# Four shared raw tiles, V and O without ones, gate weights and first mask a stage ahead, and one output product placed later

## The chip, the cores and the metric

The program runs on one core of a Trainium2 chip. The metric is the time of one execution on the device in microseconds (us), the median of three runs. The engines are called as the profile calls them: PE (TensorE, matmul), PEld (its weight loads), DVE (VectorE), ACT (ScalarE), POOL (GpSimd), SP (the queue that issues most loads and stores).

## What is computed

A trunk of two layers over 2048 positions of width 1024, all in float32. Each layer normalizes h, scales and shifts it by a modulation worked out from c, mixes, and adds gate * y to h. Layer 0 is an S5 state space beside an mLSTM; layer 1 is sliding-window attention. The change lies in layer 0 and in what it prepares for layer 1. Cut to that:

```python
def adaln(c, w, b):                      # the modulation of a layer: shift, scale, gate
    m = jax.nn.silu(c) @ w + b
    return jnp.split(m[:, None, :], 3, axis=-1)

def s5_mixer(...):                       # y is the scan's output
    return y * jax.nn.sigmoid(y @ w_glu)

def mlstm_cell(q, k, v, log_i, log_f):   # one step of the scan over chunks of 128
    b = cumsum(lf)
    d_log = where(tri, b[:, None] - b[None, :] + li[None, :], -inf)
    m_t = maximum(b + m_st, max(d_log))
    s = (q @ k.T) * exp(d_log - m_t)
    g = exp(b + m_st - m_t)
    num = s @ v + g * (q @ c_st)
    den = sum(s) + g * (q @ n_st)
    h = num / maximum(abs(den), exp(-m_t))
    c_new, n_new = decay * c_st + (w_k * k).T @ v, decay * n_st + sum(w_k * k)

def mlstm_mixer(m_in, ...):
    xc = silu(causal_conv(m_in, conv_w, conv_b))
    q, k = xc @ wq, (xc @ wk) * M_HEAD_DIM ** -0.5       # by head, 4 heads of 256
    v, o = m_in @ wv, sigmoid(m_in @ wo)
    log_i, log_f = split(concat([xc, m_in]) @ w_if + b_if)   # log_f = log_sigmoid
    h = mlstm_cell(q, k, v, log_i, log_f)
    return rmsnorm(o * h, norm_g) + skip * xc

# layer 0:  h = x + gate * (concat([y_s5, y_m * silu(m_z)]) @ w_out)
```

## The kernel before

The program is a row of stages; between two of them all engines meet (`m.clear()`), and only what has been started ahead of that crosses. Within a stage each engine runs a program of its own, written out by hand, and waits for the others by semaphores. So the order of work on an engine, and of the loads on SP's queue, is the order of the code. Every float32 product of the large ones is made as three (high by high, high by low, low by high part); to get the parts ACT casts a raw tile to its high part and DVE subtracts that from the raw tile to get the low part. This pair is called a split below. One such product of 128x512 is one MATMUL row.

**glu** takes the scan's output y and gives y * sigmoid(y @ w_glu) times a SiLU, in four blocks of 512 positions; the result goes to DRAM as `ys_d`. Its tile `g_u` holds one input. At its end SP loads the weights of dense's head 0 into `m.wide` and the inputs of dense's unit 0 into the two tiles `m.bridge`, counted by the semaphore `m.ahead`.

**dense** has 16 units, four heads by four blocks of 512 positions. Unit u does 48 products: q, k, and v beside o, in eight groups that go through four PSUM banks `e_pg`; ACT reads each result into one of four `e_stage` tiles and stores it to `cq_d`, `ck_d` or `vo_d`. A `vo_d` row holds v (256), a one, and o (256): the one makes the cell's product with v give the sum `den` too, and ACT writes it for each result (L1682). After unit u stands tile u-1: 48 products of 128 positions of `ys_d` with the first half of `ev_w_out` (L1772 to L1774, banks `e_po`), which DVE scales by the gate row `e_gate` (L1742) and adds to x (L1746); SP stores it as `h0_d`. The eight rows of that weight (512 KB each) come through two raw tiles `m.second` (`out_weight`, L1582): from the third on, each load waits until a raw tile has been split. SP's order is: four weight rows, unit 1's inputs (L1565, L1566), y (L1571), the gate chain's transfers, four weight rows, and from then on for each u: unit u+1's inputs, y, head weights, the store of tile u-2, x, the gate chain's transfers, a piece of the second layer's modulation weight `ada_w` (L1590). POOL multiplies that piece by SiLU(c) and adds it to `ada_sum` (L1634). The class `Gates` (L1385) works out the cell's decays from the gate logits in parts, one for each unit; part 2 is a long chain of small DVE instructions behind unit 2, for whose result SP waits before it goes on with unit 4's inputs.

In DVE's and ACT's programs unit u+1's splits stand ahead of tile u-1's residual. The last y (tile 15) is cast into `e_y`, the same tile that tile 14's products read, so ACT's cast waits for these (L1659), and the last product uses the banks `e_po` again, which DVE must have read.

**cell** is the mLSTM in 16 chunks of 128 positions by 4 heads. For each head PE does `first` (turns the keys, makes the scores and the product q @ state) and `second` (the state's update and scores @ v); DVE and ACT do the masking, the normalizing and the state. `turn(c)` transposes a chunk's heads, `y_part` and `blend` (DVE, ACT) make y_m of it, and `outputs(c, n)` multiplies it in 24 products with the second half of `ev_w_out` (L2272), of which each chunk has two. The eight rows of that weight come through the two tiles `m.bridge`; DVE multiplies each by the gate row (`fold`, L2154) before it is split (L1976, L2148), one for each head of chunks 0 and 1. The stage begins with 48 products by ones that sum `ada_sum` (L2279), an addition and a transpose of the second layer's gate row, which ACT copies and SP stores; the loads of weights 2 to 5 wait on SP for that. POOL makes the causal mask at the start, and for each chunk mask minus `gate_run`, of which ACT takes exps. The keys and queries of chunk 0 are loaded into `m.second` at dense's end, v and o into `m.wide`.

Chunk 0's `turn` and `outputs(0, 0)` stand in chunk 1: the turn behind `second(1, 0)`, the product behind `second(1, 2)`; DVE's blend of chunk 0 stands ahead of head 2 of chunk 1.

## Time and profile before

| what | value |
|---|---|
| median of three runs | 3034.83 us |
| the three runs | 3034.83, 3031.55, 3037.38 us |
| the profiled execution, its own time | 3025.52 us |
| its span in the trace | 3023.7 us |
| PE busy | 2765.6 us (91%) |
| DVE, ACT, POOL busy | 1558.9, 1103.1, 640.8 us |
| mean granted clock of PE | 0.957 |
| dense, from its first product to its last | 1234.8 to 1629.8 us |
| cell, first product | 1636.7 us |

The profile is of one execution. Its own time is 1.8 us more than its span, which is what lies around the span, and 9.3 us less than the median of the three runs. Busy times are sums over the span; what a change in one stage is worth has to be read from the stretch of that stage, from which engine waits there and for what. A granted clock of 1.00 is PE's full 2.4 GHz; a mean of 0.75 over a stretch is a mixture of that and of 1.2 GHz. A row of a timeline gives the start and length of an instruction (or of a run of like ones, xN), and in brackets how long its engine had been idle before it and whose end released it.

### The profile page before, as it was taken

How to read it: one execution, taken by the hardware profiler on the slowest of the kernel's cores; microseconds unless marked ns; L12 is line 12 of the kernel's file. 1: busy time of each engine (PE TensorE's matmuls, PEld its weight loads, DVE VectorE, ACT ScalarE, POOL GpSimd, SP SyncE). 2: the span in 40 equal slices, each digit the busy share in tenths (PEclk: the TensorE clock that was granted, in tenths of full speed). 3: DMA queues.
4: the chain of work that ended last, by engine and by line, in shares of the span. 5: the costliest groups of instructions: out<-in, count | busy, mean ns of one | idle time of the engine just before them, and what ended most of it. 6: DMA issues, size and time to landing. Idle time of an engine off the chain costs nothing. (4 is left out here: it accounts for less than half of the span.)

```text
span 3023.7 us, 36865 instructions
## 1 busy us (share of the span) xinstructions
PE 2765.6 (91%) x13163; PEld 2195.2 (73%) x13163; DVE 1558.9 (52%) x3227; ACT 1103.1 (36%) x2442; POOL 640.8 (21%) x526
## 2 busy tenths in 40 slices
PE   4799998999999799689997699997899999899999
PEld 2677887888888678578785577776677777667776
DVE  5565771556655456453223666664534431456664
ACT  2611221222222222334331455553522222366664
POOL 0004661544545100032232000000100000033332
PEclk7899999999999899899998899999899999999999
DMA  7216446454454465698896465662422324512221
GB/s 252 95 67 149 146 145 155 138 149 144 147 157 138 151 218 178 211 251 238 256 276 193 133 178 168 165 171 79 167 73 74 88 76 122 166 60 89 85 85 63
DMA packets 454027, 445.66 MB, mean 147 GB/s; under 512 B 157556, under 2 KB 349388, under 8 KB 450380
## 3 DMA queue, kind: packets, MB, share of 16 engines
q1 hardware_dynamic: 350340, 337.75, 38.0%
q10 hardware_dynamic: 103504, 105.54, 10.8%
q8 instruction: 106, 1.74, 0.2%
q14 instruction: 77, 0.63, 0.1%
HBM read 282.06 MB, written 162.74 MB: 147 GB/s over the span
## 5 line engine op out<-in xcount | busy, mean ns | idle before, releaser
L2771 PE MATMUL a_pg<-a_hT,a_whl 128*128 128x512 f32 x640 | 256.7, 401 | 3.4 <-DVE a_whl L878 3.4
L2772 PE MATMUL a_pg<-a_hT,a_whl 128*128 128x512 f32 x640 | 251.1, 392 | 0.0
L2773 PE MATMUL a_pg<-a_hT,a_whl 128*128 128x512 f32 x640 | 250.9, 392 | 0.0
L884 PE MATMUL p_g<-hT,w_hl 128*128 128x512 f32 x512 | 212.2, 415 | 0.0
L830 PE MATMUL pg<-hT,w_hl 128*128 128x512 f32 x512 | 206.3, 403 | 6.5 <-DVE w_hl L878 6.5
L832 PE MATMUL pg<-hT,w_hl 128*128 128x512 f32 x512 | 201.9, 394 | 0.0
L831 PE MATMUL pg<-hT,w_hl 128*128 128x512 f32 x512 | 201.7, 394 | 0.0
L886 PE MATMUL p_g<-hT,w_hl 128*128 128x512 f32 x512 | 200.2, 391 | 0.0
L885 PE MATMUL p_g<-hT,w_hl 128*128 128x512 f32 x512 | 199.8, 390 | 0.0
L2771 PEld LDWEIGHTS a_pg<-a_hT,a_whl 128*128 128x128 f32 x640 | 121.4, 190 | 42.0 <-DVE a_whl L878 11.4
L2773 PEld LDWEIGHTS a_pg<-a_hT,a_whl 128*128 128x128 f32 x640 | 121.3, 189 | 26.3
L2772 PEld LDWEIGHTS a_pg<-a_hT,a_whl 128*128 128x128 f32 x640 | 121.6, 190 | 23.6
L1074 POOL TENSOR_TENSOR s_region<-s_wt 128x512 f32<-128x512 f32 x64 | 72.5, 1133 | 299.7 <-DMA s_wt<-s5w_d 299.5
L1094 DVE TENSOR_TENSOR s_region<-p_v,s_region 128x512 f32<-128x512 f32 x64 | 44.1, 690 | 162.9 <-PE p_v L1172 154.8
L2272 PE MATMUL xp_o<-x_wout,x_yhl 128*128 128x512 f32 x256 | 108.8, 425 | 14.8 <-DVE x_wout L2148 9.6
L2920 POOL TENSOR_TENSOR shared<-shared,b_stat 128x1024 f32<-128x1024 f32 x43 | 81.5, 1896 | 184.2 <-DVE b_stat L2987 184.2
L1349 PE MATMUL g_ps<-g_gh,g_w 128*128 128x512 f32 x256 | 101.6, 397 | 19.9 <-DVE g_gh L1259 15.4
L830 PEld LDWEIGHTS pg<-hT,w_hl 128*128 128x128 f32 x512 | 97.7, 191 | 29.6 <-DVE w_hl L878 7.3
L832 PEld LDWEIGHTS pg<-hT,w_hl 128*128 128x128 f32 x512 | 97.4, 190 | 21.0
L831 PEld LDWEIGHTS pg<-hT,w_hl 128*128 128x128 f32 x512 | 97.8, 191 | 19.2
L886 PEld LDWEIGHTS p_g<-hT,w_hl 128*128 128x128 f32 x512 | 96.2, 188 | 20.7
L885 PEld LDWEIGHTS p_g<-hT,w_hl 128*128 128x128 f32 x512 | 96.4, 188 | 19.9
(502 smaller groups left out, 6848.9 us busy)
## 6 DMA issues: line engine op xcount, KB each, us to landing
s_wt<-s5w_d SPq DMA_DIRECT2D x64, 354.0 KB
vo_d<-e_stage ACTq DMA_DIRECT2D x64, 256.5 KB, 8.5
w_raw<-in_ev_w_in SPq DMA_DIRECT2D x32, 512.0 KB, 5.7
s5w_d<-gate_sums SPq DMA_DIRECT2D x32, 512.0 KB, 3.0
shared<-h_d SPq DMA_DIRECT2D x28, 512.0 KB, 4.1
arena<-in_ada_w SPq DMA_DIRECT2D x8, 1536.0 KB, 11.6
e_ada_w<-in_ada_w SPq DMA_DIRECT2D x32, 384.0 KB, 7.4
a_raw<-in_od_w_in SPq DMA_DIRECT2D x40, 256.0 KB, 3.4
```

The costliest lines, as they stand in the source:

```text
L830: nc.tensor.matmul(out, w[:, 0, k, :], x[:, 0, k, :], start=(k == 0), stop=False)
L831: nc.tensor.matmul(out, w[:, 0, k, :], x[:, 1, k, :], start=False, stop=False)
L832: last = nc.tensor.matmul(out, w[:, 1, k, :], x[:, 0, k, :], start=False, stop=(k == KC - 1))
L884: nc.tensor.matmul(out, w(0, k), x(0, k), start=(k == 0), stop=False)
L885: nc.tensor.matmul(out, w(0, k), x(1, k), start=False, stop=False)
L886: last = nc.tensor.matmul(out, w(1, k), x(0, k), start=False, stop=(k == n - 1))
L1349: nc.tensor.matmul(ps[n][:], w(0), gh[:, 0, k, :], start=(k == 0), stop=False)
L2272: mm(O[n][:], yhl[:, 0, k, :], wo[:, 0, k, cols], start=(k == 0), stop=False)
L2771: mm(bank, w[:, 0, k, :], x[:, 0, k, :], start=(k == 0), stop=False)
L2772: mm(bank, w[:, 0, k, :], x[:, 1, k, :], start=False, stop=False)
L2773: last = mm(bank, w[:, 1, k, :], x[:, 0, k, :], start=False, stop=(k == KC - 1))
L2920: nc.gpsimd.tensor_tensor(p, p, st[G % 3][:, 4].unsqueeze(2).broadcast_to([P, 4, 2 * P]), ALU.mult).then_inc(p_ready, 1)
```

## The change

- A new shared tile `four` of 128x4096 (2 MB), with the views `m.row[0..3]`, lives from glu to cell. glu uses it for `g_u`, dense for four raw rows of its output weight, then for two rows of the cell's weight (`row[2]`, `row[3]`) and chunk 0's keys and queries (`row[0]`, `row[1]`). `m.second` is gone.
- At glu's end, when the last block's `g_u` is used up, SP also loads the first four weight rows of dense. In dense the other four come in one burst once the first four are split.
- `vo_d` has no column of ones, ACT no longer writes one, and the cell loads v and o in two pieces; POOL sets the column in the tiles once. The tiles for the gate row, the `ada_w` piece and the mask are shared from dense on, and several tiles now overlie others.
- The gate chain's part 2 is cut in two, "2" and "2b"; the second is behind unit 3's splits on DVE.
- In dense's last units SP loads four rows of the cell's weight, and DVE folds the gate into them there (units 14 and 15 and behind the last y). Chunk 0's inputs are loaded in unit 14. POOL subtracts and ACT takes the exps of chunk 0's mask (`m.pm0`) at dense's end.
- The last y goes into the tile `e_x`, and the last tile's products into two `e_pg` banks, half by half, each half with a signal of its own.
- In the cell, the products by ones stand behind `first(0, 1)`, the transpose behind `first(0, 3)`, and only rows 4 to 7 of the weight are loaded and folded, through four tiles. `turn(0)` stands behind `second(1, 2)`, blend and y_part of chunk 0 at chunk 1's end, and `outputs(0, 0)` behind `second(1, 3)`, in chunk 2.

```diff
 def glu: (at the end of SP's program)
+                sp.wait_ge(pre, NB * KC)
+                for k in range(4):
+                    sp.dma_start(m.row[k], a["ev_w_out"][0, k * P:(k + 1) * P, :]).then_inc(m.ahead_w, 16)
...
 def dense:
+        ylast = xhl[:].rearrange("p q k t -> p q (k t)").rearrange("p q (k t) -> p q k t", t=P)
+        y_of = lambda t: yhl[:] if t < LASTU else ylast
+        bank = lambda t, n: (po if t < LASTU else pg)[n][:]
...
                 def out_weight(k):
-                    if k >= 2:
-                        sp.wait_ge(wo_lo, k - 1)
-                    sp.dma_start(wo_raw[k % 2][:], wov[k]).then_inc(wo_in[k % 2], 16)
+                    sp.wait_ge(wo_lo, KC // 2)
+                    sp.dma_start(wo_raw[k % 4], wov[k]).then_inc(wo_in, 16)
...
-                for k in range(KC // 2):
-                    out_weight(k)
                 unit(1)
                 y(0)
...
+                    if u in (UNITS - 4, UNITS - 3):
+                        k = u - UNITS + 4
+                        sp.dma_start(m.row[2 + k], next_wov[k]).then_inc(m.ahead_w, 16)
+                    if u == UNITS - 2:
+                        next_inputs()
+                sp.wait_ge(u_lo, 2 * UNITS)
+                for k in range(2):
+                    sp.dma_start(m.bridge[k][:], next_wov[2 + k]).then_inc(m.ahead_w, 16)
+                modulation(LASTU)
...
+                pool.wait_ge(m.ahead, 16 * 11)
+                pool.wait_ge(causal_ready, 2)
+                pool.wait_ge(gates.moved, 16)
+                nc.gpsimd.tensor_tensor(m.pm0, m.causal[:].unsqueeze(1).broadcast_to([P, MH, MC]), m.gb[:], ALU.subtract).then_inc(masked, 1)
...
                 def y(t):
                     act.wait_ge(y_in, 16 * (t + 1))
-                    if t:
+                    if t == LASTU:
+                        act.wait_ge(u_done, UNITS)
+                    elif t:
                         act.wait_ge(t_done, t)
-                    nc.scalar.copy(yhl[:, 0], y_raw[:]).then_inc(y_hi, 1)
+                    nc.scalar.copy(y_of(t)[:, 0], y_raw[:]).then_inc(y_hi, 1)
...
-                        nc.scalar.activation(s[:, HD:HD + 1], pg[g % 4][:, 0:1], ACT.Copy, scale=0.0, bias=1.0)
...
+                for h in range(MH):
+                    nc.scalar.activation(m.pm0[:, h, :], m.pm0[:, h, :], ACT.Exp, bias=m.gcol[:, 0, 0, h:h + 1]).then_inc(weighted, 1)
...
+                def fold(k):
+                    v.wait_ge(m.ahead_w, 16 * (6 if k < 2 else 8))
+                    raw = m.row[2 + k] if k < 2 else m.bridge[k - 2][:]
+                    tt(raw, raw, gate[:], ALU.mult).then_inc(folded, 1)
...
+                    if u == 2:
+                        gates.vector(v, "2b")
+                    if u >= UNITS - 2:
+                        fold(u - UNITS + 2)
                 y(UNITS - 1)
+                for k in range(2, 4):
+                    fold(k)
                 residual(UNITS - 2)
                 residual(UNITS - 1)
+                v.wait_ge(folded, 4)
...
 def cell: (PE's program)
-                pe.wait_ge(ada_ready, 1)
-                nc.tensor.transpose(O[1][0:KC, 0:P], m.ada[:, 1, 2 * KC:3 * KC], m.ident[:]).then_inc(gate_turned, 1)
                 for c in range(NMC):
                     first(c, 0)
                     if c:
                         second(c - 1, MH - 1)
+                    if c == 2:
+                        outputs(0, 0)
                     first(c, 1)
+                    if c == 0:
+                        modulation()
                     second(c, 0)
                     if c >= 2:
                         outputs(c - 2, 1)
-                    if c:
                         turn(c - 1)
...
                     second(c, 2)
-                    if c:
+                    if c == 1:
+                        turn(0)
+                    if c >= 2:
                         outputs(c - 1, 0)
```

Three places show how instructions move. First SP's queue from glu's end into dense; `UNCONDITIONAL_BRANCH` is the border of the stages, `e_y_raw` the y of tile 0, `t_bias` and `gt_d` the gate chain's. Before (the border stands right above):

```order
L1585 DMA second<-in_ev_w_out 128x1024 x4
L1565 DMA bridge<-xc_d 128x2x512
L1566 DMA bridge<-m_d 128x2x512
L1571 DMA e_y_raw<-ys_d 128x1024
L1414 DMA t_bias<-in_m_b_if 8x1
L1416 DMA gt_d<-gate_sums 8x2048
L1585 DMA second<-in_ev_w_out 128x1024 x4
L1599 DMA e_gate<-gate_d 128x1024
L1576 DMA e_h<-in_x 128x1024
L1590 DMA e_ada_w<-in_ada_w 64x1536 x2
L1565 DMA bridge<-xc_d 128x2x512
```

and after:

```order
L1323 DMA four<-in_ev_w_out 128x1024 x4
L1280 UNCONDITIONAL_BRANCH
L1564 UNCONDITIONAL_BRANCH
L1574 DMA bridge<-xc_d 128x2x512
L1575 DMA bridge<-m_d 128x2x512
L1580 DMA e_y_raw<-ys_d 128x1024
L1416 DMA t_bias<-in_m_b_if 8x1
L1418 DMA gt_d<-gate_sums 8x2048
L1593 DMA four<-in_ev_w_out 128x1024 x4
L1616 DMA gate_row<-gate_d 128x1024
L1585 DMA e_h<-in_x 128x1024
L1598 DMA ada_w<-in_ada_w 64x1536 x2
```

Four rows of the weight moved ahead of the border, and unit 1's inputs and the bias are the first loads of dense.

Second, DVE at dense's end, up to its last instruction. `e_y<-e_y_raw` is the split of the last y, the pairs on `e_up` and `e_h` are the residuals of tiles 14 and 15. Before:

```order
L1708 TENSOR_TENSOR e_y<-e_y_raw,e_y 128x1024
L1742 TENSOR_TENSOR e_up<-e_po,e_gate 128x512 x2
L1746 TENSOR_TENSOR e_h<-e_h,e_up 128x512 x2
L1708 TENSOR_TENSOR e_y<-e_y_raw,e_y 128x1024
L1742 TENSOR_TENSOR e_up<-e_po,e_gate 128x512 x2
L1746 TENSOR_TENSOR e_h<-e_h,e_up 128x512 x2
L1742 TENSOR_TENSOR e_up<-e_po,e_gate 128x512 x2
L1746 TENSOR_TENSOR e_h<-e_h,e_up 128x512 x2
```

and after, where `gate_sums` is the tile that `e_up` now overlies and `gate_row` the gate:

```order
L1771 TENSOR_TENSOR four<-four,gate_row 128x1024
L1743 TENSOR_TENSOR e_y<-e_y_raw,e_y 128x1024
L1785 TENSOR_TENSOR gate_sums<-e_po,gate_row 128x512 x2
L1789 TENSOR_TENSOR e_h<-e_h,gate_sums 128x512 x2
L1771 TENSOR_TENSOR four<-four,gate_row 128x1024
L1743 TENSOR_TENSOR e_x<-e_y_raw,e_x 128x1024
L1771 TENSOR_TENSOR bridge<-bridge,gate_row 128x1024 x2
L1785 TENSOR_TENSOR gate_sums<-e_po,gate_row 128x512 x2
L1789 TENSOR_TENSOR e_h<-e_h,gate_sums 128x512 x2
L1785 TENSOR_TENSOR gate_sums<-e_pg,gate_row 128x512 x2
L1789 TENSOR_TENSOR e_h<-e_h,gate_sums 128x512 x2
```

Four folds (L1771) came in, two of them between the last split and the residuals, the last split writes `e_x`, and the last residual reads `e_pg` banks.

Third, PE at the cell's start. `xp_ks` and `xp_bb` are `first`, `xp_c` and `xp_aa` are `second`, `xp_o<-ones` the products by ones. Before:

```order
L2279 MATMUL xp_o<-ones,ada_sum 128x1 x24
L2284 MATMUL xp_o<-ident,ada 8x128
L2226 MATMUL xp_ks<-ident,second 128x128 x2
L2228 MATMUL xp_ks<-second 128x128 x2
L2235 MATMUL xp_bb<-x_c,second 128x257 x2
L2226 MATMUL xp_ks<-ident,second 128x128 x2
L2228 MATMUL xp_ks<-second 128x128 x2
L2235 MATMUL xp_bb<-x_c,second 128x257 x2
L2245 MATMUL xp_c<-wide,x_kw 128x257
```

and after:

```order
L2287 MATMUL xp_ks<-ident,four 128x128 x2
L2289 MATMUL xp_ks<-four 128x128 x2
L2298 MATMUL xp_bb<-x_c,four 128x257 x2
L2287 MATMUL xp_ks<-ident,four 128x128 x2
L2289 MATMUL xp_ks<-four 128x128 x2
L2298 MATMUL xp_bb<-x_c,four 128x257 x2
L2343 MATMUL xp_o<-ones,ada_sum 128x1 x24
L2308 MATMUL xp_c<-wide,x_kw 128x257
L2309 MATMUL xp_c<-wide,x_kw 128x257
L2313 MATMUL xp_aa<-wide,x_st 128x257
```

The products by ones moved behind the second `first`, and the transpose (L2284 before) has left this stretch.

## Rows read from the trace of the kernel before

**Rows 1.** Windows, all engines: window, its length, busy (x instructions) by engine, clock, DMA.
```profile
1234.80:1295.00 60.20, 39.44 (x150) 31.64 (x151) 21.88 (x19) 24.37 (x47) 6.17 (x2) 0.81 0.77 246
1295.00:1629.80 334.80, 322.53 (x1391) 264.87 (x1390) 116.90 (x152) 122.58 (x274) 95.42 (x30) 0.98 0.85 242
1642.50:1716.00 73.50, 40.46 (x163) 31.73 (x164) 41.45 (x91) 30.78 (x75) 5.68 (x3) 0.74 0.59 178
```

**Rows 2.** Timeline of PE in dense: its first instruction after each wait.
```profile
1260.80 0.79 PE L1772 MATMUL e_pg<-e_x,e_wh 128*128 128x512 f32 x1 [12.54 <-DVE e_x L1708]
...
1292.39 0.80 PE L1772 MATMUL e_pg<-e_x,e_wh 128*128 128x512 f32 x1 [8.22 <-DVE e_x L1708]
...
1318.37 0.50 PE L1772 MATMUL e_pg<-e_x,e_wh 128*128 128x512 f32 x1 [1.41 <-DVE e_x L1708]
...
1476.65 0.79 PE L1772 MATMUL e_pg<-e_x,e_wh 128*128 128x512 f32 x1 [4.23 <-DVE e_x L1708]
...
1616.04 0.77 PE L1772 MATMUL e_po<-e_wout,e_y 128*128 128x512 f32 x1 [5.97 <-DVE e_up L1742]
```

**Rows 3.** DMA issues of 1380 to 1600: KB each, median us to landing.
```profile
bridge<-m_d SPq DMA_DIRECT2D x9, 512.0 KB, 12.3
```

**Rows 4.** Timeline of DVE at glu's end.
```profile
1215.59 1.16 DVE L1277 TENSOR_TENSOR g_o<-g_s,g_z 128x512 f32<-128x512 f32 x1 [3.63 <-DMA ys_d<-g_o]
```

**Rows 5.** Timelines of SP, DVE and ACT at dense's start.
```profile
1231.17 13.97 SPq L1585 DMA_DIRECT2D second<-in_ev_w_out  x4
...
1258.19 1.27 DVE L1453 TENSOR_SCALAR gate_sums<-gate_sums,t_bias 8x2048 f32<-8x2048 f32 x1 [3.76 <-DMA t_bias<-in_m_b_if]
...
1272.75 0.86 SPq L1565 DMA_DIRECT2D bridge<-xc_d  x1
...
1288.75 1.04 ACT L1648 CAST e_x<-bridge 128x1024 fp32r<-128x1024 f32 x1 [10.31 <-DMA bridge<-m_d]
```

**Rows 6.** Timelines at dense's end and the border to cell.
```profile
1610.16 1.04 ACT L1659 CAST e_y<-e_y_raw 128x1024 fp32r<-128x1024 f32 x1 [9.99 <-PE e_po L1774]
...
1611.24 3.46 DVE L1708 TENSOR_TENSOR e_y<-e_y_raw,e_y 128x1024 fp32r<-128x1024 f32 x1 [14.06 <-ACT e_y L1659]
...
1630.05 1.29 DVE L1742 TENSOR_TENSOR e_up<-e_po,e_gate 128x512 f32<-128x512 f32 x2 [10.90 <-PE e_po L1774]
...
1613.69 4.30 POOL L1634 TENSOR_TENSOR ada_sum<-ada_sum,e_ada_w 128x1536 f32<-128x1536 f32 x1
...
1636.72 5.28 PE L2279 MATMUL xp_o<-ones,ada_sum 64*128 64x1 f32 x48 [6.71 <-PEq L148]
```

**Rows 7.** Timelines of DVE, ACT and PE in cell's first two chunks.
```profile
1660.86 1.23 DVE L2154 TENSOR_TENSOR bridge<-bridge,x_gate 128x1024 f32<-128x1024 f32 x1 [5.86 <-DMA bridge<-in_ev_w_out]
...
1690.97 2.15 DVE L2126 SCALAR_TENSOR_TENSOR x_y<-xp_o,cols,x_xs 128x128 f32<-128x128 f32 x8
...
1695.43 1.23 DVE L2138 TENSOR_TENSOR x_yhl<-x_y,x_yhl 128x1024 fp32r<-128x1024 f32 x1
...
1664.54 0.42 ACT L1991 ACTIVATE x_ha<-x_hs 128x256 f32<-128x256 f32 x1 [10.06 <-DVE x_hs L2104]
...
1670.84 0.42 ACT L1991 ACTIVATE x_ha<-x_hs 128x256 f32<-128x256 f32 x1 [0.61 <-DVE x_hs L2104]
...
1707.98 0.76 PE L2272 MATMUL xp_o<-x_wout,x_yhl 128*128 128x512 f32 x1 [9.64 <-DVE x_wout L2148]
...
1727.46 0.60 PE L2260 MATMUL xp_o<-ident,x_hs 128*128 128x128 f32 x4
```

**Rows 8.** Windows over one chunk each, in the cell's middle.
```profile
1757.32:1783.00 25.68, 24.14 (x122) 19.80 (x121) 16.14 (x50) 15.24 (x38) 1.89 (x2) 1.00 0.63 177
1860.06:1886.83 26.77, 24.14 (x122) 19.79 (x121) 17.22 (x50) 15.24 (x38) 1.26 (x1) 1.00 0.56 170
```

**Rows 9.** Timelines of SP and ACT: unit 10's second input.
```profile
1457.23 0.70 SPq L1566 DMA_DIRECT2D bridge<-m_d  x1
...
1474.29 1.04 ACT L1648 CAST e_x<-bridge 128x1024 fp32r<-128x1024 f32 x1 [8.97 <-DMA bridge<-m_d]
```

252 lines of the change are left out of this document (146 added, 106 removed).

## The prediction

> **What bounds the kernel now.** I read the windows by stage first, then TensorE's (PE's) timeline, then what the engine that released it was doing. PE carries the program; the three stages that the change touches are glu (up to 1231) [rows 5], dense (1234.8 to 1629.8) and cell (from 1636.7). In dense PE is busy 322.5 of 334.8 us once it runs, but only 39.4 of its first 60.2 us, and 40.5 of the 73.5 us with which cell begins, at granted clocks of 0.81 and 0.74 where dense's middle has 0.98 [rows 1]. So there is nothing to win in the middle and much at two starts. PE's own idle stretches are few and long: 12.5, 8.2, 1.4, 4.2 and 6.0 us in dense [rows 2]. The other input is DMA: its share is 0.85 over dense's middle [rows 1], and a 512 KB input takes 12.3 us to land there [rows 3].
>
> **glu's end.** Four loads of 512 KB (rows of the output weight) go onto SP's queue behind those that are there. VectorE already waited 3.6 us for a store to land while such loads ran [rows 4]; 2 MB more prolong that by 6 to 8 us, and the last stores are then each late. I charge +1 us (0 to +4): two output tiles stand between VectorE and these stores and take up part of the delay, and a second wait as long as the one that is there is the upper end.
>
> **dense's start.** Before, SP spends 14.0 us on four weight loads, because two raw tiles must come free in turn, and only then issues unit 1's inputs; four more weights follow before unit 2's [rows 5]. Behind the first set stands also the bias, for which VectorE waits at 1258.2 [rows 5] ahead of unit 1's splits. PE finishes unit 0 at 1248.3 (1260.80 less 12.54) and starts unit 1 at 1260.8 [rows 2]. After, unit 1's inputs leave once unit 0's are split, near 1236, and are in before unit 0 ends. ScalarE (ACT), which must fit four weight casts between eight results, I put 1 us behind PE; the last result (0.8), a cast (1.0) and a split (1.2) follow, and PE goes on near 1252.7: a wait of 4.5 us. The last four weights now come in one burst that starts near 1250.5 and lands near 1259, and ACT stands before it with seven results behind it; PE has four banks in hand, so I charge 2.5 us (0 to 5). Unit 1 and tile 0 took 23.4 us (1260.80 to 1284.17), and unit 2 then waited 8.2 us for inputs issued at 1272.75, which landed 16 us later behind the weights [rows 2, 5]. After, these are issued near 1254.5 with 2 MB less ahead of them and land by 1268. Unit 2 starts at 1248.3 + 4.5 + 23.4 + 2.5 = 1278.7 and not at 1292.4: -13.7. A wait also costs a slow restart: tile 15 took 14.0 us from 1616.04 to 1630.05 [rows 2, 6] against 10.9 at full clock (1344 products from 1292.39 to 1610.07, less waits and restarts, 0.228 each, 48 to a unit or tile), so 3.1; unit 1 and tile 0 together show 1.6. For the restart that goes I take 2.4. Sum -16.1 (-10 to -19).
>
> **The gate chain.** In unit 2 the second part (about 7 us of small instructions) moves behind unit 3's splits. Unit 3's wait of 1.4 us [rows 2] goes. But SP stands at the store of this chain's result until it is done, and unit 4's inputs are queued behind: issued near 1309, needed by 1319. I charge +1 (0 to +5). Sum -0.4. Unit 10's wait (4.2) [rows 2] has none of its causes touched: 0 (-6 to 0).
>
> **The last units.** Rows of the next stage's weight (0.5 MB each) go into units 12 and 13, its chunk 0 inputs (2.2 MB) into unit 14, two rows more behind unit 15. Dense's DMA is busy 0.85 [rows 1], a unit moves some 5.3 MB (242 GB/s by 21.8 us), so 0.5 MB delay a landing by about 1.6 us. Of the units after unit 2 only unit 10 waited over 2 us [rows 2], so most have some time in hand. Cost 0 (0 to +6).
>
> **dense's end.** ACT waits 10.0 us for tile 14 before it can cast the last y, PE then waits 6.0 us [rows 2, 6]. After, the last y goes into the tile of unit 15's inputs and the last product into other banks: both are free long before, so PE goes on at 1610.1: -6.0, and its restart goes, -3.1. The last product is done half by half; one scaling (0.6) is hidden: -0.6. What is late next? The addition loads now stand behind two 0.5 MB rows, then GpSimd (POOL) adds (4.3) [rows 6], makes the mask (1.4), ACT does exps (2.6): about 1626 in before's clock, where the last store lands near 1627. Cover is 1 us thin: +1 (0 to +4). Sum -8.7.
>
> One thing speaks against this term: VectorE's last split took 3.46 us while POOL added, against 1.23 for an instruction of its size in cell [rows 6, 7], and the last two folds (two SBUF operands each) now stand in that place. At this row's excess of 2.2 each the sum would have +4.5. I take it as a rival, since tile 15's 10.9 us give the folds room. The Trainium skill, "SBUF — State Buffer", section "SBUF: two separate sides", says that VectorE's and GpSimd's shared port pair is an exclusive lock and the loser blocks for the whole instruction; by that rule the sum would have one POOL instruction's length for every fold that comes second. The row agrees that there is a price, though it is shorter than the POOL addition beside it.
>
> **cell's start**, in t from the stage's first PE instruction (1636.72). Before, 48 products by ones, an addition and a transpose (5.8 us) precede all else; the first output product starts at t = 71.3, the second ends at t = 90.7 [rows 7]. VectorE paces it. Its heads follow at 6.3 us where fold, split and cast of a weight chain through ACT (1664.54 to 1670.84), and it stands 5.9 us for a weight load (1660.86) [rows 7], as the two raw tiles and SP's wait for the gate row hold the loads back. After: the mask, its exps and four folds are done in dense; POOL's memsets hold the first bank product until t = 2.2; the ones-products stand behind first(0,1) and end near 10.6, so head 0 is put out at 13.8. Then, by my count of each head's instructions, the heads: 5.2 (no fold), 6.3, 5.0, 6.3, 8.3 (with chunk 0's normalisation), 5.2, so t = 50 for the seventh. The last weight split (1.2) and the blend with its cast and split (1690.97 to 1696.66, 5.7) [rows 7] give t = 57 for the first output product, by which time first(2,0) and second(1,3) are done. It runs 7.0 with its restart, then 2.8 of recurrence and 5.6 of the second product: t = 72.4. -18.3 (-11 to -22). The moved loads of weights 4 to 7 leave SP at t = 10 and 22 and are needed at 22 and 33, with landings of 6 to 8 us: hidden. The split vo load adds one issue (0.8 us) to an SP queue that waits most of the time: 0.
>
> **cell's middle.** Chunks take 25.7 us, or 26.8 when POOL's subtraction meets VectorE (DVE busy 16.1 or 17.2) [rows 8]. The phase may shift either way: 0 (-6 to +6).
>
> **The sum**: +1 - 16.1 - 0.4 - 8.7 - 18.3 = -42.5. Against the profiled span of 3023.7 that is 2981.2, and 2983.0 for its own time of 3025.5. That run is 9.3 below the median of the runs shown, so I forecast 3034.8 - 42.5 = 2992.3 for a median.
>
> **Rivals.**
> - *Dense is bound by DMA.* For: share 0.85, over 1 in stretches. If bytes and not waits set the stage, its gain goes and glu's and cell's stay: -17, 3018. Against: PE does run 1295 to 1629.8 at 322.5 busy, and after it needs only 9% more rate. 0.12.
> - *The early work only moves the chain.* ACT's hand-overs, not loads, set cell's first two chunks: only the 5.8 at the head and the 5.9 wait less 5.8 of ones-products are saved, -6 in place of -18.3: 3004. For: the 6.3 pace has no DMA in it. Against: seven heads at 5 to 8 us still end by 50. 0.10. Both of these together give 3029, within 0.2%: 0.03.
> - *VectorE held up by POOL* in the last two folds, as above, +4.5: 2997. For: the row of 3.46. Against: nothing waits for these folds until cell's first output product. 0.05.
> - *Slower: input landings in dense.* One mechanism: loads packed closer in time make each unit's input late, as unit 10's was (ACT waited 9.0 us for it, and it landed 17.1 us after its issue) [rows 9]. Price 4.2 of idle and 2.4 of restart, 6.6; on twelve units 79, less 42.5: 3071. It decides from seven such units on, that is when the median landing of 12.3 us [rows 3] passes about 17. Against: only one unit in fourteen did. 0.05.
>
> **Numbers.** Forecast 0.65, about 2974 to 3010 by itself. Each case but the last two is faster by over 0.2%, about what a measurement can tell from no change: faster 0.92, same 0.03, slower 0.05. The range reaches over the bounds of start and cell (-61 would need all best ends) and up to the DMA case: 2974 to 3018.
>
> **What would show it.** PE's idle before unit 1 near 4.5 us and none before unit 2; no idle before tile 15; cell's first output product at t = 57, waiting for the split of y and not for a weight; dense's length 371 and not 402. Wrong if unit inputs are waited for in several units, if POOL's or ACT's last work ends dense, or if glu ends over 4 us later.

## The result, and the profile after

The changed kernel takes 2991.7 us (median, 2991.0 to 2998.3) where the kernel before took 3036.1 beside it. The ratio worked out from all runs is 0.9865, interval 0.985 to 0.988; that of the two medians is 0.9854. The forecast was 2992.3. The profiled execution of the changed kernel has a time of its own of 2991.0 and a span of 2989.2, so the two traces shown differ by 34.5 us, and the medians by 44.4. The forecast's sum was made against the first of these. The total is therefore nearer than its terms deserve, and the terms are what follows.

Each stretch below is taken from PE's timelines, from the start of one product to the start of another, so that it doesn't matter that the changed run was already 2.0 us late before glu's first product.

| stretch | before | after | difference | forecast |
|---|---|---|---|---|
| glu's first product to dense's first | 192.7 | 193.9 | +1.2 | +1 |
| to unit 3's first product | 83.6 | 65.8 | -17.8 | -17.5 |
| unit 3 to unit 5 | 43.7 | 52.2 | +8.5 | +1 |
| unit 5 to unit 9 | 88.4 | 87.7 | -0.7 | 0 |
| unit 9 to unit 11 | 50.6 | 43.5 | -7.1 | 0 |
| unit 11 to unit 15 | 87.1 | 87.1 | 0 | 0 |
| unit 15 to dense's last product | 41.5 | 33.0 | -8.5 | -9.7 |
| to the cell's first product | 7.1 | 10.3 | +3.2 | +1 |
| to the end of the second output product | 90.7 | 71.8 | -19.0 | -18.3 |
| to the last chunk's output product | 370.2 | 372.5 | +2.3 | 0 |
| everything else | | | +3.4 | 0 |

Of the +3.4 of everything else 2.0 stand ahead of glu's first product and 1.4 behind the last chunk's output product.

The windows over the same places as [rows 1] (window, its length, then busy time and count of PE, PEld, DVE, ACT and POOL, granted clock, DMA share, GB/s):

```profile
1237.98:1298.20 60.22, 54.16 (x216) 43.54 (x217) 34.04 (x38) 28.63 (x50) 12.64 (x4) 0.90 0.87 290
...
1280.00:1607.60 327.60, 319.96 (x1402) 263.38 (x1402) 153.79 (x160) 122.35 (x221) 98.23 (x30) 0.99 0.86 260
...
1617.50:1691.00 73.50, 57.47 (x270) 46.60 (x271) 44.20 (x115) 35.72 (x85) 5.82 (x6) 0.80 0.64 175
```

In dense's first 60 us PE is busy 54.2 and not 39.4, at a clock of 0.90 and not 0.81; at the cell's start it is 57.5 and not 40.5. PE's timeline, the first instruction behind each of its long waits (start, length, instruction, and the wait with its releaser), answers to [rows 2, 6, 7]:

```profile
1256.97 0.80 PE L1822 MATMUL e_pg<-e_x,e_wh 128*128 128x512 f32 x1 [5.19 <-DVE e_x L1743]
...
1332.68 0.79 PE L1822 MATMUL e_pg<-e_x,e_wh 128*128 128x512 f32 x1 [6.90 <-DVE e_x L1743]
...
1617.51 0.66 PE L2287 MATMUL xp_ks<-ident,four 128*128 128x128 f32 x2 [9.88 <-PEq L148]
...
1673.42 0.79 PE L2335 MATMUL xp_o<-x_wout,x_yhl 128*128 128x512 f32 x1 [6.62 <-DVE x_yhl L2197]
```

Unit 1 waits 5.2 us (12.5 before), units 2, 3 and 10 and tile 15 don't wait. Two waits are new or longer: 6.9 ahead of unit 4, and 9.9 at the border to the cell, where there were 6.7. The first output product comes 55.9 us behind the cell's first product and waits for the split of y.

**Unit 4.** Its chain in the timelines of SP and ACT (`mx_d` is the store of the gate chain's part 2, `bridge` the inputs):

```profile
1312.04 0.65 SPq L1426 DMA_DIRECT2D mx_d<-t_ends  x1
...
1314.65 0.47 SPq L1575 DMA_DIRECT2D bridge<-m_d  x1
...
1329.33 1.05 ACT L1677 CAST e_x<-bridge 128x1024 fp32r<-128x1024 f32 x1 [13.74 <-DMA bridge<-m_d]
```

SP issued unit 4's inputs only after the store for whose data it had stood, they landed 14.7 us later, and PE, idle from 1325.8, wanted them 3.5 us before ACT could begin to cast them.

**The border.** DVE and POOL at dense's end; the last product starts at 1607.2:

```profile
1603.85 6.79 DVE L1789 TENSOR_TENSOR e_h<-e_h,gate_sums 128x512 f32<-128x512 f32 x2
1610.84 1.29 DVE L1785 TENSOR_TENSOR gate_sums<-e_pg,gate_row 128x512 f32<-128x512 f32 x2 [0.20 <-DVE e_h L1789]
...
1603.50 2.75 POOL L1656 TENSOR_TENSOR ada_w<-ada_w,c_silu 128x1536 f32<-128x1536 f32 x1 [8.88 <-DMA ada_w<-in_ada_w]
1606.33 3.76 POOL L1659 TENSOR_TENSOR ada_sum<-ada_sum,ada_w 128x1536 f32<-128x1536 f32 x1
1610.05 1.71 POOL L1663 TENSOR_TENSOR gate_sums<-causal,gate_run 128x512 f32<-128x512 f32 x1
```

The two additions of tile 14's residual take 6.8 us beside POOL's two instructions, 1.3 without such company (in combo2, below). So the last residual starts 3 us later than the last product allows, and with it the last store.

### The profile page after: what moved, and what is told of

The parts are those of the page before. It is cut to its first block and busy times, and to the rows that moved or that the text cites. A ratio compares the mean times of both kernels' runs of the same rounds, so it can differ in the third digit from the quotient of the medians.

```text
span 2989.2 us, 36821 instructions
## 1 busy us (share of the span) xinstructions
PE 2758.0 (92%) x13163; PEld 2190.9 (73%) x13163; DVE 1586.3 (53%) x3227; ACT 1099.1 (37%) x2378; POOL 640.4 (21%) x528
## 3 DMA queue, kind: packets, MB, share of 16 engines
q8 instruction: 106, 1.74, 0.2%
## 5 line engine op out<-in xcount | busy, mean ns | idle before, releaser
L2844 PEld LDWEIGHTS a_pg<-a_hT,a_whl 128*128 128x128 f32 x640 | 121.7, 190 | 26.4
L831 PEld LDWEIGHTS pg<-hT,w_hl 128*128 128x128 f32 x512 | 97.8, 191 | 19.1
L886 PEld LDWEIGHTS p_g<-hT,w_hl 128*128 128x128 f32 x512 | 96.5, 189 | 20.8
## 6 DMA issues: line engine op xcount, KB each, us to landing
ada_w<-in_ada_w SPq DMA_DIRECT2D x32, 384.0 KB, 8.2
```

Source lines behind the costliest of these rows:

```text
L831: nc.tensor.matmul(out, w[:, 0, k, :], x[:, 1, k, :], start=False, stop=False)
L886: last = nc.tensor.matmul(out, w(1, k), x(0, k), start=False, stop=(k == n - 1))
L2844: last = mm(bank, w[:, 1, k, :], x[:, 0, k, :], start=False, stop=(k == KC - 1))
```

## The experiments

All are edits of the changed kernel, but for the last. Medians were taken with the kernel before at 3042 to 3046 us in these comparisons, where the result had 3036, and the changed kernel was not timed again beside them; so stretches of the traces are compared first. "Dense" is from its first product to the cell's first: 402.0 before, 379.5 after.

One trace of each has a scatter of its own. Three of the experiments below leave dense's code alone (pool_phase, output_old, ones_first), and their dense is 380.3, 381.5 and 382.1; so 379.5 is the low end of a band of 2.6 us, and a difference of that size shows nothing. At the cell's start, the seven traces with the changed kernel's code there have the first output product at t = 53.9 to 55.9 from the cell's first product, and the second's end at 70.3 to 72.1.

**s_behind: SP's store of the chain behind unit 4's inputs.**

```diff
                     if u + 1 < UNITS:
                         unit(u + 1)
+                    if u == 3:
+                        gates.transfers(sp, 2)
                     y(u)
...
-                    gates.transfers(sp, u)
+                    if u != 2:
+                        gates.transfers(sp, u)
```

> The changed kernel, with one edit: the store that waits for the gate chain's part 2 is issued by SP behind unit 4's inputs and not ahead of them. In the changed kernel PE waits 6.9 us ahead of unit 4 (1332.68). Theory (SP's order): its inputs left SP only at 1314.0, since SP stood at that store until VectorE's chain was done at 1312; with the edit they leave near 1305, the wait is gone, and with its restart dense is 8 to 10 us shorter (about 370 from its first to the cell's first product, where the changed kernel has 379.5). Rival (bytes): these inputs needed 15 us to land because the queues are full; leaving earlier they land hardly earlier, a wait of 4 us or more stays, and dense gains under 3 us.

Dense 378.2, median 2991.5 (2986.1 to 2996.0): 1.3 us less than 379.5, which is no more than the scatter, and not 8 to 10. Unit 4 does not wait any more, so the cause was named rightly; but its price came back one step later, which neither theory had. PE, then DVE and POOL:

```profile
1317.87 0.77 PE L1825 MATMUL e_po<-e_wout,e_y 128*128 128x512 f32 x1 [5.26 <-DVE gate_sums L1788]
...
1304.54 7.88 DVE L1469 SCALAR_TENSOR_TENSOR t_w<-t_w 64x128 f32<-64x128 f32 x7
...
1304.98 2.77 POOL L1659 TENSOR_TENSOR ada_w<-ada_w,c_silu 128x1536 f32<-128x1536 f32 x1 [10.24 <-DMA ada_w<-in_ada_w]
1307.84 3.50 POOL L1662 TENSOR_TENSOR ada_sum<-ada_sum,ada_w 128x1536 f32<-128x1536 f32 x1
```

Tile 2 waits for the residual of tile 1, which stands behind the chain on DVE, and the chain is long: seven instructions take 7.9 us while POOL works, and the same seven take 2.2 in the changed kernel, where SP's stall had kept POOL's data away by chance:

```profile
1306.85 2.19 DVE L1469 SCALAR_TENSOR_TENSOR t_w<-t_w 64x128 f32<-64x128 f32 x7
```

**chain_whole: part 2 in one piece again.**

```diff
                     gates.vector(v, u)
+                    if u == 2:
+                        gates.vector(v, "2b")
...
-                    if u == 2:
-                        gates.vector(v, "2b")
```

> The changed kernel with the gate chain's part 2 in one piece again, behind unit 2's work, as before the change. Theory (the cut trades one wait for another): the chain ends near 1306 and not 1312, unit 4's inputs leave 6 us earlier and its wait of 6.9 falls to about 0 to 1; but unit 3's splits come 7 us later and unit 3 waits about 7: dense 379.5 give or take 2. Rival (the cut is a gain by itself and unit 4 waits for something else): 7 to 10 us longer. Second rival (the cut is a loss by itself, since VectorE has time in hand in unit 2): 7 us shorter.

Dense 377.7, median 2993.7. Unit 3 waits 5.3 us, unit 4 not at all: the cut in two traded one wait for another, as the first theory said; what it was worth by itself is too little to see here (1.8 us).

**chain_slot3: both queues cleared.**

```diff
                     gates.vector(v, u)
+                    if u == 3:
+                        gates.vector(v, "2b")
...
-                    if u == 2:
-                        gates.vector(v, "2b")
...
                     x(u)
-                    gates.transfers(sp, u)
+                    if u == 3:
+                        gates.transfers(sp, 2)
+                    if u != 2:
+                        gates.transfers(sp, u)
```

> The changed kernel with the gate chain's second piece one unit later on VectorE (behind the residual of tile 1, ahead of unit 4's splits) and SP's store of its result behind unit 3's loads, so that neither unit 4's inputs nor tile 2's residual stand behind it. With the store alone moved (s_behind) unit 4's wait of 6.9 us went, but tile 2 then waited 5.3 us for a residual behind the chain, whose row of seven instructions took 7.9 us while POOL added the modulation. Theory (two queues, SP's and VectorE's, have to be cleared both): no wait over 2 us in units 3 to 5 and their tiles, dense 7 to 9 us shorter than 379.5. Rival (the chain costs wherever it stands, since POOL's instructions hold it): a wait of 4 to 6 us ahead of unit 4, whose splits are now behind it, dense within 2 us of 379.5.

Dense 373.4, 6.2 us shorter and clear of the scatter; median 2987.4 (2985.3 to 2988.4). Units 3 to 5 and their tiles don't wait; two waits of 1.1 and 1.2 us turned up later in the stage. The chain itself was not disturbed there (L1469 took 2.2 us); POOL fell on the residual ahead of it, whose two additions took 7.0 us, and there DVE had the time.

**mod_early: the modulation one unit earlier from unit 8 on.**

```diff
-                    if u > 1:
-                        modulation(u - 1)
+                    if 1 < u < UNITS // 2:
+                        modulation(u - 1)
+                    if u == UNITS // 2:
+                        modulation(u - 1)
+                        modulation(u)
+                    if u > UNITS // 2:
+                        modulation(u)
...
-                modulation(LASTU)
                 store(UNITS - 2)
```

> The changed kernel with the pieces of the second layer's modulation weight loaded one unit earlier from unit 8 on, so that POOL has nothing of it left to do at dense's end. In the changed kernel VectorE's two additions of tile 14's residual take 6.8 us beside POOL's last two instructions, the last residual starts at 1610.8, 3 us behind PE's last product, and from that product to the cell's first one 9.9 us pass (before: 6.7). Theory (VectorE is held up by POOL at dense's end): the additions take 1.3 to 2.5 us and 9.9 falls to about 6.5, dense 3 us shorter. Rival (the mask's subtraction and its exps end the stage): 9.9 falls by 1 at most, unless these come earlier too; then the last store alone is left and both theories meet, and the length of the two additions tells them apart.

The border fell from 9.9 to 6.1 us and the two additions to 1.3, as the first theory has it. Still the kernel lost: dense 384.0, median 2999.1. Two pieces one behind the other made SP wait until POOL had used the first, and unit 9's inputs stood behind that:

```profile
1421.16 16.75 SPq L1598 DMA_DIRECT2D ada_w<-in_ada_w  x4
```

PE then waited 5.2 us ahead of unit 9 (at 1451.64). This was my own edit, and it repeats the mistake of the prediction: a wait on SP is paid by what is queued behind it.

**pool_phase: POOL's mask subtraction in each of the cell's chunks 7 us later.**

```diff
                     if c >= 2:
-                        pool.wait_ge(st_ready, seq(c - 1, 0))
+                        pool.wait_ge(hs_ready, seq(c - 1, 1) + 1)
```

> The changed kernel with POOL's mask subtraction of each chunk of the cell released by head 1's output of the chunk ahead and not by head 0's mask product, so about 7 us later in the chunk, where VectorE is idle for 2 us. In the changed kernel a chunk takes 26.1 to 26.8 us (from 1707.94 to 2024.75: twelve chunks, 26.4 each); before, four chunks took 25.7. Theory (the phase of POOL's subtraction against VectorE's split of y makes the difference): all chunks take about 25.7, the cell is 7 to 9 us shorter. Rival (the chunk is paced by PE or by ACT): no change within 2 us.

Every chunk but the last takes 25.67 us, the stretch from the cell's first product to the last chunk's output product is 8.0 us shorter (436.3 and not 444.3), and the median is 2983.1 (2981.1 to 2985.6). Windows of one chunk each, first two of the changed kernel and then two of pool_phase (columns as above):

```profile
1761.17:1787.25 26.08, 24.13 (x121) 19.79 (x121) 16.52 (x50) 15.24 (x39) 1.27 (x1) 1.00 0.57 172
1787.25:1813.53 26.28, 24.40 (x121) 19.87 (x121) 16.74 (x50) 15.24 (x39) 2.06 (x1) 1.00 0.56 171
```

```profile
1761.37:1787.04 25.67, 24.14 (x121) 19.80 (x121) 16.13 (x50) 15.24 (x39) 1.29 (x1) 1.00 0.56 170
1787.04:1812.71 25.67, 24.13 (x120) 19.79 (x121) 16.14 (x50) 15.23 (x39) 1.30 (x1) 1.00 0.59 177
```

PE, PEld and ACT are busy as long as before; DVE is busy 16.1 and not 16.5 to 16.7, and the chunk is shorter by that and no more. In the changed kernel POOL's instruction stood on the split of y:

```profile
1773.43 1.63 DVE L2197 TENSOR_TENSOR x_yhl<-x_y,x_yhl 128x1024 fp32r<-128x1024 f32 x1
...
1772.70 1.27 POOL L2021 TENSOR_TENSOR x_pm<-causal,gate_run 128x512 f32<-128x512 f32 x1 [24.81 <-DVE x_st L2138]
```

The split takes 1.6 us there and 1.2 alone.

**rows_late: the first four weight rows at dense's start and not at glu's end.**

```diff
-                sp.wait_ge(pre, NB * KC)
-                for k in range(4):
-                    sp.dma_start(m.row[k], a["ev_w_out"][0, k * P:(k + 1) * P, :]).then_inc(m.ahead_w, 16)
...
+                for k in range(4):
+                    sp.dma_start(m.row[k], a["ev_w_out"][0, k * P:(k + 1) * P, :]).then_inc(m.ahead_w, 16)
                 unit(1)
```

> The changed kernel with the first four rows of dense's output weight loaded at dense's start, ahead of unit 1's inputs, and not at glu's end (four raw tiles all the same, so SP does not wait between them). Theory (dense's start: what stands ahead of unit 1's inputs costs, at 2 MB by 240 to 300 GB/s some 7 to 8 us): unit 1's wait, 5.2 in the changed kernel, becomes 9 to 13, glu ends about 1 us earlier, and dense is 5 to 9 us longer than its 379.5. Rival (the four tiles alone are the gain, since they take SP's 14.0 us of waiting away): unit 1's wait stays within 2 us of 5.2 and the total within 2 us.

Unit 1's wait is 7.0 us and not 5.2; it starts 20.8 us behind unit 0, where the changed kernel has 19.0 and the kernel before 26.0. So of 7.0 us won there the four tiles alone give 5.2, and glu's end is 0.6 shorter. For the wait that is the rival's case. For the total it is not: dense came out at 385.7, 6.2 us longer, which is the theory's number; median 2996.9. The waits of 7.7 ahead of unit 4 and of 10.4 at the border are no explanation, since the four traces with unchanged dense have 6.9 to 8.7 and 9.9 to 10.7 there. Of the 3.6 us beyond their longest dense, unit 1 has 1.8; for the rest I have no mechanism.

**last_tile_old: the last y and product in e_y and e_po.**

```diff
-        y_of = lambda t: yhl[:] if t < LASTU else ylast
+        y_of = lambda t: yhl[:]
-        bank = lambda t, n: (po if t < LASTU else pg)[n][:]
+        bank = lambda t, n: po[n][:]
...
                 def y(t):
-                    if t == LASTU:
-                        act.wait_ge(u_done, UNITS)
-                    elif t:
+                    if t:
                         act.wait_ge(t_done, t)
```

> The changed kernel with the last y and the last product in the tiles and banks of before (e_y, e_po, the halves not apart). Theory (the term of dense's end, 6.0 of idle, 3.1 of restart, 0.6 of a scaling): PE waits about 6 us ahead of tile 15 again and tile 15 takes 14.0 and not 10.9; of this 9 the part that was covered by POOL's and DVE's late work at the border (9.9 us there, 6.7 before) comes back, so dense is 5 to 9 us longer than 379.5. Rival (the border is set by POOL's last piece and the exps in any case): under 3 us longer.

Dense 388.8, 9.3 us longer, median 3000.9. The wait ahead of tile 15 is 10.7 us and not the 6 of before, since the folds, whose weight rows landed only at 1605.4, now stand ahead of the residual that frees the bank:

```profile
1605.39 2.36 DVE L1769 TENSOR_TENSOR bridge<-bridge,gate_row 128x1024 f32<-128x1024 f32 x2 [4.27 <-DMA bridge<-in_ev_w_out]
...
1609.09 0.77 PE L1818 MATMUL e_po<-e_wout,e_y 128*128 128x512 f32 x1 [10.69 <-DVE gate_sums L1781]
```

The folds at dense's end are free only with the other banks; the two edits belong together.

**output_old: chunk 0's turn, blend and first output product where they were.**

```diff
-                    if c == 2:
-                        outputs(0, 0)
                     first(c, 1)
...
-                    if c == 1:
-                        turn(0)
-                    if c >= 2:
+                    if c:
                         outputs(c - 1, 0)
```

(and DVE's and ACT's parts of it likewise)

> The changed kernel with chunk 0's turn, blend and first output product where they stood before (the product behind second(1, 2)); all else as changed. The changed kernel has its first output product 55.9 us and the end of the second 71.8 us behind the cell's first product. Theory (most of the cell's 19 us comes from what is no longer done at its start, and the move gives some 4 to 6 of them, since before it PE held first(2, 0) and second(1, 3) behind a product that waited for the last weight): the second product ends 4 to 6 us later than 71.8. Rival (only the move makes the gain possible): 10 us or more later. Second rival (the move gives nothing, VectorE paces all): within 1.5 us.

The first output product comes at t = 52.9, but the second ends at 74.5 and not 71.8: the move is worth 2.8 us, less than I had set. Median 2995.2.

**fold_in_cell: rows 0 to 3 loaded early, but folded in the cell.**

```diff
-                    if u >= UNITS - 2:
-                        fold(u - UNITS + 2)
...
-                        if 2 <= k < 6:
-                            fold(k + 2)
+                        if k + 1 < KC:
+                            fold(k + 1)
```

> The changed kernel with rows 0 to 3 of the cell's weight loaded in dense as changed, but multiplied by the gate row in the cell, one for each head as before; dense's VectorE has no folds. Theory (VectorE paces the cell's start: each of the four folds stands in it): the first output product comes 4 to 5 us later than 55.9 (three folds of 1.2 and the first one with its cast behind it), and dense's end is not shorter, since its folds were hidden. Rival (the folds at dense's end cost there too, VectorE beside POOL): dense 1 to 3 us shorter, so that the total is nearly the same.

The first output product comes 59.2 us behind the cell's first and not 55.9, the end of the second is 3.6 later; dense is 380.1, no shorter. Median 2999.7. The folds are hidden in dense and on the path in the cell. The trace also shows that they only settle which additions meet POOL at the border: without them tile 14's two took 1.3 us, but tile 15's took 4.1 beside POOL's last addition, and the wait there was still 9.0.

**ones_first: the products by ones ahead of the cell again.**

```diff
+                modulation()
+                pe.wait_ge(ada_ready, 1)
                 for c in range(NMC):
                     first(c, 0)
...
-                    if c == 0:
-                        modulation()
                     second(c, 0)
```

> The changed kernel with the 48 products by ones and the addition of the modulation ahead of everything in the cell, as before the change (the transpose stays behind first(0, 3)). Theory (these 5.8 us are put off the path by the move, since VectorE waits for POOL's memsets and ACT's casts there anyway for 2 to 3 us): first output product 3 to 6 us later than the 55.9 of the changed kernel. Rival (before as after they are on the path, as head 0's output at 13.1 against 15.1 shows little gain): under 2 us later.

First output product at t = 56.7 (55.9), second's end at 73.2 (71.8); median 2998.1, with dense 2.6 us longer in this trace for reasons that the edit doesn't touch. The rival holds: of the 5.8 us that I saw ahead of all else, 0.8 to 1.5 were worth something, and these are hardly more than the scatter. If the three edits on the cell don't overlap, the experiments add up to 3.6 + 2.8 + 1.5 = 7.9 of its 19.0 us. The other 11 are left over, and I put them down to what was not tried apart: the loads that no longer wait for two raw tiles and for the gate row (waits of 5.9 and 2.5 us of DVE in the trace of before), and chunk 0's mask and exps.

**combo2: chain_slot3, pool_phase and the modulation early without the stall.**

```diff
-                    if u > 1:
+                    if 1 < u <= 8:
                         modulation(u - 1)
...
                     y(u)
+                    if u == LASTU:
+                        modulation(LASTU)
...
+                    if 8 <= u < LASTU:
+                        modulation(u)
...
-                modulation(LASTU)
                 store(UNITS - 2)
```

(beside the diffs of the other two)

> chain_slot3 and pool_phase together, and the modulation's pieces loaded one unit earlier from unit 8 on without SP waiting for POOL (each at its unit's end, the last one behind the last y), so that POOL is done before dense's end. Theory: 8.8 us from the cell's chunks (25.67 each), 7 to 9 from units 3 to 5 and about 3.8 from the border to the cell (9.9 to 6.1), 2970 to 2974 in all. Rival (a wait that goes is followed by the next one): the chunks' 8.8 alone, about 2983.

2973.4 us (2971.4 to 2982.7), a ratio to the kernel before of 0.977 (0.9753 to 0.9787). The 0.9865 of the change was taken against a faster series of the kernel before (3036 and not 3046), so the two ratios overstate the difference; the medians themselves differ by 18.3 us, the spans of the two traces by 18.4. PE has one long wait left in dense, and then the border:

```profile
1258.80 0.79 PE L1828 MATMUL e_pg<-e_x,e_wh 128*128 128x512 f32 x1 [5.19 <-DVE e_x L1749]
...
1608.78 0.66 PE L2293 MATMUL xp_ks<-ident,four 128*128 128x128 f32 x2 [6.11 <-PEq L148]
```

Dense is 368.8 us, 10.7 less than the changed kernel, and the cell up to the last chunk's output product 436.0 and not 444.3. This version beats both.

**before_again: the kernel before once more, for a second trace.**

> The kernel before once more, for a second trace: its profiled execution of 3025.5 us was the shortest of those seen, the others lie between 3031 and 3056. Theory (unit inputs in dense land late in some executions): the extra 10 to 25 us stand in dense as waits of PE for DMA. Rival (the phase of POOL against VectorE in the cell): the chunks of 25.7 are 26.4. Second rival (clock): no stage has them, all stages are longer in proportion.

Its profiled execution took 3047.7 us, with a span of 3045.9: 22.2 more than the trace shown. Of these 15.0 stand in dense (417.0), 3.7 ahead of glu, 0.7 in glu and 3.1 in the cell. Units 9 and 11 wait:

```profile
1464.52 0.79 PE L1772 MATMUL e_pg<-e_x,e_wh 128*128 128x512 f32 x1 [3.77 <-DVE e_x L1708]
...
1517.94 0.79 PE L1772 MATMUL e_pg<-e_x,e_wh 128*128 128x512 f32 x1 [6.91 <-DVE e_x L1708]
```

From unit 5 to unit 15 this execution takes 238.1 us, the one shown 226.1, the changed kernel 218.3. In eleven of the twelve traces of the changed kernel and its edits that stretch takes 218.2 to 219.6; the twelfth is mod_early with the wait that it made itself. So the gap between 34.5 and 44.4 is, as far as one more trace can tell, mostly here: the kernel before loses more in dense's middle in other executions than in its fastest, and the changed kernel doesn't.

**Why dense's middle became calm.** The DMA view of 1380 to 1540 (q1 is SP's queue, q10 ACT's: packets, MB, share of 16 engines; then KB each and median us to landing) of before:

```profile
q1 hardware_dynamic: 9286, 24.50, 57.9%
q10 hardware_dynamic: 7669, 13.97, 29.8%
...
vo_d<-e_stage ACTq DMA_DIRECT2D x28, 256.5 KB, 9.9
...
bridge<-m_d SPq DMA_DIRECT2D x7, 512.0 KB, 12.7
...
e_y_raw<-ys_d SPq DMA_DIRECT2D x7, 512.0 KB, 14.3
```

and of the changed kernel:

```profile
q1 hardware_dynamic: 10033, 26.78, 58.3%
q10 hardware_dynamic: 8779, 15.99, 27.8%
...
vo_d<-e_stage ACTq DMA_DIRECT2D x30, 256.0 KB, 3.5
...
e_y_raw<-ys_d SPq DMA_DIRECT2D x8, 512.0 KB, 4.6
...
bridge<-m_d SPq DMA_DIRECT2D x7, 512.0 KB, 9.0
```

ACT's queue, which holds the stores of q, k and v|o, moves 14% more bytes in less engine time: 1.74% of the window for a MB and not 2.13. A store of `vo_d` lands in 3.5 us and not 9.9, and what is queued beside lands earlier too: y in 4.6 and not 14.3. The only thing that the change does to these stores is the column of ones: a row had 513 numbers, 2052 bytes, and has 512. In all twelve traces of kernels without the column the median landing of `vo_d` over the whole stage is 3.6 to 4.3 us, in both with it 8.5 and 9.6 (there the profile has a landing for only half of these stores).

The packets in the traces say more, since those of 2052 bytes can be told from the rest by their size. In dense of the kernel before, ACT's queue moves 8192 of them and 8192 of 2048 bytes, from the same staging tiles. The first take 114 ns on average and the others 89 (118 and 88 in the second trace); the medians are alike (85 and 84), and the difference is in a tail: 3.9% of the first take over 300 ns, 0.2% of the others. In the twelve traces without the column all 16384 have 2048 bytes and take 88 to 90. So these stores are dearer within one and the same execution.

That this is what PE then waited for is an inference. The waits themselves follow late inputs: the second input of units 9, 10 and 11 landed after 11.3, 17.0 and 12.3 us in the trace of before (unit 10 waits), after 15.6, 11.1 and 19.1 in before_again (units 9 and 11 wait) and after 8.1, 5.9 and 9.4 in the changed kernel. But the median over the whole stage for that input is 11.5 and 9.7 in the two traces with the column and 8.1 to 9.5 without, much closer than for the stores, and no kernel changed the column alone.

The Trainium skill, "DMA: Bandwidth & Descriptors", section "How a descriptor splits into AXI transactions", says that a descriptor which doesn't start on a 256-byte boundary reads from the boundary below and pays for bytes that it doesn't use. Rows of 2052 bytes behind one another start off that boundary nearly always. The direction agrees with the trace; but the page states it of reading, and here the rows off the boundary are those that are written, and that the cost would be as large as measured the page doesn't say.

## Why the prediction was right, and where it was not

- **glu's end**, +1: 1.2 in the trace. The other traces with this end of glu take 194.2 to 195.8 and not 193.9, the kernel before 192.7 and 193.5, so the usual cost is nearer to 2. Inside the range of 0 to 4.
- **dense's start**, -16.1 with unit 3's -1.4: 17.8 to unit 3's start. Unit 1's wait was to be 4.5 and is 5.2, unit 2's was to go and went. The step read from SP's queue (what stands ahead of unit 1's inputs) held. What rows_late adds: nearly all of unit 1's part is from four tiles in place of two, and little from the loads in glu.
- **The gate chain**, +1 (0 to +5): 8.5 from unit 3 to unit 5, of which 6.9 is idle. The mechanism was named (SP stands at the store, unit 4's inputs behind it); the term was mis-sized. I put the inputs' issue at 1309 and the need at 1319; in the trace these are 1314 and 1326. The step that failed is the time between: +1 stands for 11 us from the issue to PE's start, and they were 18.7, of which the landing of the second input took 14.7. The prediction's own rows had a landing of 16 us for unit 2's inputs, and it didn't use them here. s_behind and chain_whole showed that both the store on SP and the chain on DVE have to get out of the way, and that POOL sets how long the chain is.
- **The last units**, 0, and **unit 10's wait**, 0 (-6 to 0): -7.1 between units 9 and 11, just beyond that range. "None of its causes touched" was wrong: that wait had a late input as its cause, and in the changed kernel inputs in dense's middle land earlier. The sum had no term for the column of ones, whose bytes are the likeliest reason (the packets above), though not a tried one. The price of the weight rows was put too low on the way (0.5 MB at the 242 GB/s named are 2.1 us and not 1.6), but no unit waited for them.
- **dense's end**, -8.7: -8.5 and +3.2, together -5.3. The wait and the restart went as worked out. "Cover is 1 us thin" was right to worry, but POOL's last piece did not end the stage itself; it held VectorE's residual of tile 14 for 5.5 us. The rival with this mechanism named the folds; the folds ran in 2.4 us for two, and the price fell on the additions behind them, 3 us and not 4.5. Without the folds (fold_in_cell) it fell on tile 15's additions. With POOL done early (combo2, mod_early) the border is 6.1.

  The Trainium skill, "SBUF — State Buffer", section "SBUF: two separate sides", has the rule for it, a lock held for the whole instruction, where VectorE's has two SBUF inputs. The rows agree: 6.8 us for two additions beside 6.5 us of POOL, 1.3 without.
- **The cell's start**, -18.3: -19.0. First output product forecast at t = 57 and measured at 55.9, the second's end at 72.4 and 71.8; heads at 13.1 and then 5.2, 6.4, 3.9, 6.3, 8.6 and 5.2 apart, where I counted 13.8 and 5.2, 6.3, 5.0, 6.3, 8.3, 5.2. Counting each head's instructions on VectorE was the best step of the prediction. Its story for the first 5.8 us was not: ones_first puts that at 0.8 to 1.5. And 11 of the 19.0 us are not taken apart by any run, so here the size of the term is shown and its parts only in part.
- **The cell's middle**, 0 (-6 to +6): +2.3. Before, the first chunks ran at 25.7 and the later ones at 26.3 on average; after, the average was 26.4 from the start. pool_phase shows the cause that I had named and not priced.
- **The sum**: -42.5 against -34.5 between the traces. The misses, +7.5 at units 3 to 5, -7.1 at unit 10, +2.2 and +1.2 at the end, +2.3 in the cell and +3.4 elsewhere, add up to 9.5 us, and smaller ones take 1.5 of it back. The median came out within 1 us all the same. The other executions of the kernel before are slower than the one that I worked from, and the one of them that was traced lost most in waits like unit 10's, which the changed kernel doesn't have; the forecast held these waits to be untouched. So that the total fits to 1 us was luck.

Of the rivals, the one of DMA in dense was nearest to something real, with the sign reversed: the middle did hang on landings, and they got shorter. The early work in the cell did more than move the chain, and in dense's middle input landings didn't get later.

## What to carry to other kernels

When a step is put elsewhere on an engine, look for what is queued behind it on that engine and, where another queue waits for its result, behind that wait too: clearing one of two only hands the wait on. Give an edit that changes the length of a row in memory a line in the sum of its own, even where the bytes stay nearly the same, and look for it in the durations of single packets before any landing time. And where VectorE paces a loop, put GpSimd's instructions where VectorE is idle, or, as the rows below suggest and no run tried, beside its instructions that read PSUM; here one changed wait gave 8 us.

One trace of each kernel can't carry a difference of 1 or 2 us. Traces with the same code in a stage give that stage's scatter for nothing.

## What the runs showed of the hardware that I had not expected

- POOL's instructions stop those of VectorE that read two SBUF tiles almost wholly: seven of 64x128 that take 2.2 us took 7.9 beside 6.3 us of POOL (s_behind), two additions of 128x512 took 6.8 and 7.0 in place of 1.3. Those that read a PSUM bank and one SBUF tile are not held up at all. In dense of the changed kernel, 15 scalings from `e_po` began during one of POOL's modulation instructions and took 0.68 us each, as alone; 14 additions of the same size, from two SBUF tiles, had a median of 2.8 in place of 0.68. The trace of before shows both in a row, beside POOL's addition of 1613.69 to 1617.99:

```profile
1614.62 1.27 DVE L1742 TENSOR_TENSOR e_up<-e_po,e_gate 128x512 f32<-128x512 f32 x2
1615.82 3.33 DVE L1746 TENSOR_TENSOR e_h<-e_h,e_up 128x512 f32<-128x512 f32 x2
```

- Stores of 128 rows of 2052 bytes landed in 8.5 to 9.6 us (median), of 2048 bytes in 3.6 to 4.3. Within one trace a packet of 2052 bytes took 114 or 118 ns on average and one of 2048 took 88 or 89. The loads of y in the same stage have a median landing of 12.3 and 10.8 us with the first and 5.5 to 8.3 with the second.
- Two traces of the kernel before differ by 22 us (3025.5 and 3047.7), 15 of them in dense; of the waits for late inputs in dense's middle the first has one (4.2 us) and the second two (3.8 and 6.9). One trace didn't show what the median contained.
